# Big starts 32 bytes later, and the slots of the back end's weight ring lie 16 bytes apart within 64 bytes

## What is computed

```python
y = jnp.concatenate([y_rwkv, y_gla], axis=-1) @ w_out[i]
h = h + rms_norm(y, norm_mix_post[i])
hn = rms_norm(h, norm_ffn_pre[i])
f = (jax.nn.silu(hn @ ffn_gate[i]) * (hn @ ffn_up[i])) @ ffn_down[i]
h = h + rms_norm(f, norm_ffn_post[i])
e = p[i] @ ple_proj[i]
gate = jax.nn.sigmoid(h @ ple_gate[i] + ple_gate_b[i])
h = h + rms_norm(gate * e, norm_ple[i])
...
h = short_conv_mixer(h, conv_w_in[j], conv_w[j], conv_w_out[j])
x = x + g_m[:, None, :] * rms_norm_2(h, norm_gains[i, 1])
h = modulate(rms_norm_2(x, norm_gains[i, 2]), sh_f, sc_f)
h = swiglu(h, ffn_w_gate_up[i], ffn_w_down[i])
```

## Time and profile before

| | |
|---|---|
| median of 3 runs | 3021.24 us (3016.89 to 3022.47) |
| span of the profiled execution | 3020.5 us |
| TensorE (PE) busy | 2871.8 us, 95% of the span |
| weight loads (PEld) busy | 2352.7 us, 78% |
| VectorE (DVE), ScalarE (ACT) busy | 1470.8 us, 1157.3 us |
| mean granted clock of TensorE | 0.976 of full |

### The profile page before, as it was taken

One profiled execution on the slowest core, in us unless ns is written; L12 is line 12 of the kernel. 1 busy time (PEld: TensorE's weight loads), 2 busy tenths in 40 slices (PEclk: granted clock), 3 DMA queues, 4 the chain that ended last, 5 costly groups with the idle time before them and its releaser, 6 DMA issues.

```text
span 3020.5 us, 57113 instructions
## 1 busy us (share of the span) xinstructions
PE 2871.8 (95%) x25216; PEld 2352.7 (78%) x25216; DVE 1470.8 (49%) x2060; ACT 1157.3 (38%) x1945; POOL 261.0 (9%) x304
## 2 busy tenths in 40 slices
PE   5987999788998999999999999999999999999997
PEld 4776677788885878888888888788888888888886
DVE  5669675455455645332443337675455534244323
ACT  4776664222224443222322235432244323233322
POOL 2000123544440000000000000000000000000000
PEclk9997899899998999999999999999999999999998
DMA  4320344211102232222222232222222222233322
GB/s 140 132 73 4 115 146 149 59 39 37 37 15 78 84 119 91 98 94 95 93 96 92 97 112 91 84 91 97 98 91 93 96 97 94 95 98 123 95 96 84
DMA packets 100437, 273.08 MB, mean 90 GB/s; under 512 B 9120, under 2 KB 36384, under 8 KB 100192
## 3 DMA queue, kind: packets, MB, share of 16 engines
q1 hardware_dynamic: 91408, 236.94, 23.9%
q0 software_dynamic: 8784, 32.51, 3.3%
HBM read 256.69 MB, written 12.58 MB: 89 GB/s over the span
## 4 chain that ended last, share of the span: by engine, by line
PE 66%; DVE 2%; ACT 1%; issue 0%; DVEq 0%; ACTq 0%
PE be_ps L2997 48%; PE be_ps L3050 16%; PE be_ps L3063 1%; DVE be_ring L2776 1%; PE be_ps L2721 1%; PE be_ps L2715 0%; PE be_ps L2400 0%; DVE be_raw_r L3245 0%; ACT be_whi L3100 0%; DVE be_total L2734 0%; DVE big L2748 0%; DVE big L2758 0%; DVE ext_r L2786 0%; DVE big_r L2786 0%; PE be_ps L2439 0%
## 5 line engine op out<-in xcount | busy, mean ns | idle before, releaser
L3245 DVE TENSOR_TENSOR be_raw_r<-be_raw,be_whi 128x1024 fp32r<-128x1024 f32 x361 | 442.4, 1225 | 974.9 <-ACT be_whi L3100 974.5
L3100 ACT CAST be_whi<-be_raw 128x1024 fp32r<-128x1024 f32 x361 | 379.0, 1050 | 893.1 <-DMA be_raw<-in_ffn_down 316.7
L2997 PE MATMUL be_ps<-ext_r,be_whi 128*128 128x512 f32 x2304 | 713.5, 391 | 6.8 <-DVE be_raw_r L3245 3.5
L2997 PE MATMUL be_ps<-big_r,be_whi 128*128 128x512 f32 x2048 | 642.1, 394 | 0.8 <-DVE be_raw_r L3245 0.5
L2997 PEld LDWEIGHTS be_ps<-ext_r,be_whi 128*128 128x128 f32 x2304 | 430.2, 188 | 102.3 <-DVE be_raw_r L3245 4.8
L2997 PEld LDWEIGHTS be_ps<-big_r,be_whi 128*128 128x128 f32 x2048 | 382.9, 188 | 96.1 <-DVE big_r L2784 1.0
L2997 PE MATMUL be_ps<-ext_r,be_raw_r 128*128 128x512 f32 x1152 | 448.4, 389 | 0.0
L2997 PE MATMUL be_ps<-big_r,be_raw_r 128*128 128x512 f32 x1024 | 408.0, 398 | 0.0
L3050 PE MATMUL be_ps<-ext_r,be_whi 128*128 128x512 f32 x1152 | 354.7, 389 | 0.0
L2997 PEld LDWEIGHTS be_ps<-ext_r,be_raw_r 128*128 128x128 f32 x1152 | 216.3, 188 | 45.4
L3050 PEld LDWEIGHTS be_ps<-ext_r,be_whi 128*128 128x128 f32 x1152 | 216.2, 188 | 44.8
(11 more groups left out here) (350 smaller groups left out, 3833.9 us busy)
## 6 DMA issues: line engine op xcount, KB each, us to landing
be_raw<-in_ffn_gate SPq DMA_DIRECT2D x88, 512.0 KB, 3.5
be_raw<-in_ffn_up SPq DMA_DIRECT2D x88, 512.0 KB, 3.5
be_raw<-in_ffn_down SPq DMA_DIRECT2D x88, 512.0 KB, 3.5
be_raw<-in_conv_in SPq DMA_DIRECT2D x48, 512.0 KB, 3.5
gp_ada<-in_ada POOLq DMA_DIRECT2D x24, 512.0 KB, 3.7
rp_ada<-in_ada POOLq DMA_DIRECT2D x24, 512.0 KB, 4.4
rwkv_prepared<-big SPq DMA_DIRECT2D x16, 512.0 KB, 3.2
be_raw<-in_w_out SPq DMA_DIRECT2D x16, 512.0 KB, 3.5
```

Source lines behind the costliest of these rows:

```text
L2997: mm = pe.matmul(ps[:, bank], part[:, k * P:(k + 1) * P], xs(k), start=(k == order[0] and i == 0), stop=(k == order[-1] and i == 2))
L3100: act.copy(w.hi[:, n % 3], w.raw[:, n % 3]).then_inc(w.hi_ready, 1)
L3245: dve.tensor_tensor(w.lo(n), w.raw[:, n % 3], w.hi[:, n % 3].bitcast(F32), ALU.subtract).then_inc(w.lo_ready, 1)
```

## The change

Two tensors of 8 numbers (32 bytes) are put in, one ahead of `big` and one behind `c`. `big` so begins at place 32. What lies behind `c` moves on by 64 bytes and keeps its place; `gains`, `mod` and `c`, between the two, move by 32.

`be_raw` and `be_whi` become flat tensors of 3 * 1024 + 8 numbers, whose slot n begins at number 1028 n instead of 1024 n, that is 16 bytes further for each slot. `be_raw` begins at place 32, so its slots (the low weights) are at places 32, 48 and 0. It is now 12320 bytes long, 32 more than a multiple of 64, so `be_whi` begins at place 0, and its slots (the high weights) are at places 0, 16 and 32. No instruction, wait or transfer is added, removed or moved.

```diff
     def __init__(self, core, ctx, a):
-        self.raw, self.low = two_views(core, ctx, "be_raw", [P, 3, D])
-        self.hi = ctx.enter_context(core.nc.sbuf_tensor("be_whi", [P, 3, D], F32R))
+        raw, low = two_views(core, ctx, "be_raw", [P, 3 * D + 8])
+        hi = ctx.enter_context(core.nc.sbuf_tensor("be_whi", [P, 3 * D + 8], F32R))
+        self.raw, self.low, self.hi = ([t[:, (D + 4) * n:(D + 4) * n + D] for n in range(3)] for t in (raw, low, hi))
...
-        return self.low[:, n % 3]
+        return self.low[n % 3]
...
-                    sp.dma_start(w.raw[:, n % 3] if dst is None else dst, src).then_inc(w.loaded[n % 3], 16)
+                    sp.dma_start(w.raw[n % 3] if dst is None else dst, src).then_inc(w.loaded[n % 3], 16)
...
-                    for i, (part, xs) in enumerate(((w.hi[:, slot], x[0]), (w.hi[:, slot], x[1]), (w.lo(slot), x[0]))):
+                    for i, (part, xs) in enumerate(((w.hi[slot], x[0]), (w.hi[slot], x[1]), (w.lo(slot), x[0]))):
...
         core.const = ctx.enter_context(nc.sbuf_tensor("const", [P, N_STAY * P], F32))
+        core.pad_big = ctx.enter_context(nc.sbuf_tensor("pad_big", [P, 8], F32))
         big, big_r = two_views(core, ctx, "big", [P, 2 * 20, HALF])
...
         c = ctx.enter_context(nc.sbuf_tensor("c", [P, KD], F32))
+        core.pad_ext = ctx.enter_context(nc.sbuf_tensor("pad_ext", [P, 8], F32))
```

More of the change, by code:

```diff
@@ L2800, in __init__ @@
     def __init__(self, core, ctx, a):
-        self.raw, self.low = two_views(core, ctx, "be_raw", [P, 3, D])
-        self.hi = ctx.enter_context(core.nc.sbuf_tensor("be_whi", [P, 3, D], F32R))
+        raw, low = two_views(core, ctx, "be_raw", [P, 3 * D + 8])
+        hi = ctx.enter_context(core.nc.sbuf_tensor("be_whi", [P, 3 * D + 8], F32R))
+        self.raw, self.low, self.hi = ([t[:, (D + 4) * n:(D + 4) * n + D] for n in range(3)] for t in (raw, low, hi))
         self.loaded = [core.sem(f"be_loaded{s}") for s in range(3)]
         self.hi_ready, self.lo_ready = core.sem("be_hi_ready"), core.sem("be_lo_ready")
-        self.ahead = Ahead([(a["w_out"][n], self.raw[:, n], self.hi[:, n], self.lo(n), self.loaded[n], self.hi_ready,
+        self.ahead = Ahead([(a["w_out"][n], self.raw[n], self.hi[n], self.lo(n), self.loaded[n], self.hi_ready,
                              self.lo_ready) for n in range(3)])
     def lo(self, n):
-        return self.low[:, n % 3]
+        return self.low[n % 3]
 def back_end(core, a, z, y_gla, big, big_r, ext, ext_r, w, gains, out):
@@ L2950, in _ @@
                         tiles = a["ple_proj"][4 * (i - 2):4 * (i - 1)].rearrange("a p k -> p a k")
-                        load(n, tiles, w.raw[:, n % 3].rearrange("p (a k) -> p a k", a=4))
+                        load(n, tiles, w.raw[n % 3].rearrange("p (a k) -> p a k", a=4))
                     else:
@@ L3048, in swiglu @@
                             enter(n, m)
-                        for i, (part, x) in enumerate(((w.hi[:, slot], hi), (w.hi[:, slot], lo), (w.lo(slot), hi))):
+                        for i, (part, x) in enumerate(((w.hi[slot], hi), (w.hi[slot], lo), (w.lo(slot), hi))):
                             mm = pe.matmul(ps[:, m], part[:, m * P:(m + 1) * P], x, start=(j == 0 and i == 0),
@@ L3061, in embedding @@
                         at = slice((2 * g + k) * P, (2 * g + k + 1) * P)
-                        for i, (part, x) in enumerate(((w.hi[:, slot], p_hi), (w.hi[:, slot], p_lo), (w.lo(slot), p_hi))):
+                        for i, (part, x) in enumerate(((w.hi[slot], p_hi), (w.hi[slot], p_lo), (w.lo(slot), p_hi))):
                             mm = pe.matmul(ps[:, steps.bank[n, g]], part[:, at], x[:, k, cols(half)],
@@ L3099, in weight @@
                     act.wait_ge(w.loaded[n % 3], 16 * (n // 3 + 1))
-                    act.copy(w.hi[:, n % 3], w.raw[:, n % 3]).then_inc(w.hi_ready, 1)
+                    act.copy(w.hi[n % 3], w.raw[n % 3]).then_inc(w.hi_ready, 1)
             def take(n, g, dst, y_free):
@@ L3244, in weight @@
                     dve.wait_ge(w.hi_ready, n + 1)
-                    dve.tensor_tensor(w.lo(n), w.raw[:, n % 3], w.hi[:, n % 3].bitcast(F32), ALU.subtract
+                    dve.tensor_tensor(w.lo(n), w.raw[n % 3], w.hi[n % 3].bitcast(F32), ALU.subtract
                                       ).then_inc(w.lo_ready, 1)
```

## The result

The changed kernel takes 3033.43 us (median of 4 runs, 3031.30 to 3036.89) against 3019.06 us before (4 runs). The ratio is 1.0051, with a 95% interval from 1.0035 to 1.0066: slower by half a per cent, where I had forecast 2998.3 us.

The account below looks back on a forecast made before the run. TensorE, busy 95% of the span, was taken to bound the kernel by its large matmuls' pace. 3020.5 - 22.9 (`big`) + 0 (small matmuls) + 0 (ring slots) = 2997.6 us, plus 0.7 gives 2998.3 us; range 2977 to 3037 us.

Parts of the forecast that it names:

- What bounds the kernel: From about 950 us on, the back end runs at the pace of TensorE's large matmuls, with almost no idle time.
- Part 1: Back end, `big` to place 32: 3456 large matmuls go from 233.35 to 226.73 ns, 22.9 us less.
- Part 2: Back end, new places of the ring's weight slots: 226.73 ns in all slots, so 0 us.
- the first theory: Large matmuls: the stall belongs to the moving stream's own place, weights' place costs nothing, 226.73 ns in all slots.
- some form of distance: Large matmuls, distance from x to weights sets the pace: below 3015 us (0.20), 3015 to 3027 (0.09), up to 3037 (0.29).
- the place of `big` alone: Back end: only the place of `big` counts, the weights' places cost nothing, 2998 us; chance 0.30.
- Distance counts, and quarter distances are bad: Back end: distances of 16 or 48 are slow, mean pace 231.14 ns, 15.7 us more, 3036.9 us; chance 0.29.
- the third rival: Large matmuls: places don't count, the paces belong to each tensor's memory region or bank; time stays 3021.2 us; chance 0.12.
- The half clock: Large matmuls at 1.2 GHz: 426 ns each, stall gone, which halves to a floor of 213 ns at full clock.
- The cover of the ring: Back end, transfers and copies into the ring's new places: some 5.3 us of delay are hidden, so nothing put down.
- the small matmuls that read `big`: 16 other groups, 92 us together: up to 2.7 us either way, taken as 0, 3 us kept for the range.

Follow-up runs that it names:

- part 1 alone: The kernel before with only `big` moved to place 32 and all ring slots left at place 32: 3005.18 us against 3021.26 us, ratio 0.9941.
- the kernel with level distances: The kernel before with `big` moved 160 bytes and `ext` 256, plain ring, weights a multiple of 256 bytes from x: 3001.72 us against 3021.70 us, ratio 0.9929.
- the second map: No kernel, only float32r matmuls: distance stepped by 16 bytes from 0 to 496 in three random orders, then five kernels' settings; 233.3 ns at 160, 228.9 at 192.

## Why the prediction was wrong

**What bounds the kernel** was right: the back end lives by the pace of its large matmuls, and the whole effect of the change is in that pace.

**Part 1** failed in its premise that 32 bytes make `big` like `ext`. I had two paces and two places, 0 and 32, and counted places within 64 bytes because the change is made of 16s and 32s. The trace showed no period at all. `big` had in fact been 160 of 256 bytes from the weights, and went to 192: 228.9 ns, not 226.73, so 15.4 us and not 22.9. Nearly all of the 22.9 us is to be had (21.2 us in the back end, 3001.72 us in all), but takes 160 bytes.

**Part 2** failed in the term that I put at 0, and this is what turned the sign. Of the ends I took 226.73 ns, on the ground that most matmuls had it. That ground was bad: those 5280 had it because each of their distances was 0, and the change ended just that. The weights' place isn't free; it cost `ext` 4.7 ns on 5280 matmuls, 24.8 us, and `big` the difference between 228.9 and 231.7 ns on 3456, 9.7 us. With the 15.4 us of part 1 taken off, that makes 19.1 us more, against 18.9 us by the mean spacing and 17.1 us in the back end. My sentence that a change of `ext` without a move of its own would refute the first theory came true. By my own chances some form of distance had 0.58 (0.20, 0.09 and 0.29) and the place of `big` alone 0.30, and yet the forecast followed the latter.

**The rivals.** "Distance counts, and quarter distances are bad" had the right cause, at 0.29 almost the equal of the forecast's 0.30. Its mean pace of 231.14 ns and its 3036.9 us lie close to the 231.6 ns and 3033.4 us measured, and that is partly luck. It counts within 64 bytes, and it adds up load by load: so it has slots 0 and 2 at 231.1 and 228.9 ns, and they have 231.7 and 231.8 with x in `ext`. The region of memory, the third rival, is excluded by part 1 alone and by the kernel with level distances. The two rules of the Trainium skill that the prediction sets beside it foretold neither pace: the lines of 16 bytes (SBUF — State Buffer, Specifications (TRN2)) don't tell distances of 64 or 160 bytes from 0, and the weight loads that take no bandwidth from the running matmul (TensorE: Matmul & The Clock Gate, Step-by-step) give the weights' place no say, where the runs have 226.7 to 233.3 ns by it.

**The half clock.** I argued from the earlier trace rows that the stall is gone there. That row couldn't show it: by their sizes its x and weights are level, so it has no distance to compare. The start of the second map, at distance 48, bears the sentence out.

**The cover of the ring** held: 3.5 us to land over all slots, and no wait at L2998 that wasn't there before (6.6 us of idle time against 6.8 us). If the small matmuls that read `big` changed, I can't tell it from the front end's spread of 10 us.

**What stays open** is the mechanism. The stall was seen in float32r streams alone and at the full clock alone, depends on where x and weights lie within 256 bytes, and doesn't shrink with the load; the lowest pace grows with the moving columns. Why 256, why a sixteenth, and what picks one of two paces at some distances, no run here tells. Nor was it tried whether a matmul without any weight load beside it would be free of the stall.

## What to carry to other kernels

In a long stream of float32r matmuls with 512 moving columns and loads of 128, put x (high and low) and the weights (high and low) at the same place within 256 bytes, here a multiple of 32; it was worth 0.7% of this kernel for 256 bytes of padding. For another shape measure first: with 256 moving columns the same place was the slower one (120.0 against 113.3 ns). A period must be measured before an offset is chosen by it: a short program of nothing but the matmuls, with the places stepped, gives the whole map in one run and repeats the kernel's paces within 0.7 ns. Where a resource's present state is already the best one (distance 0 for 60% of the matmuls), a change of it can hardly gain, and its pace is no estimate for the state after.

## What the runs showed of the hardware that was not expected

- One and the same float32r matmul of 512 columns takes 226.7 to 236.5 ns at full clock, by the places of its operands alone; in bfloat16 it takes 215.8 ns at all four places tried.
- Two distances that are equal within 64 or 128 bytes differ: 0 has 226.7 ns, 64 has 233.3, 128 has 232.1 to 233.7. 256 more changes the mean by 0.5 ns at most, apart from the distances with two paces.
- At some distances the stream has two paces, such as 233.3 and 226.9 ns at 144.
- At the half clock none of this is seen: 427 ns at distance 48, as at 0.
- The best distance goes with the shape: 0 with 512 moving columns, 64 or 192 with 256 (113.3 to 113.5 ns, against 120.0 at 0), both with loads of 128 columns.
